# Splitting the 512-column matmuls of the weight products into two of 256 columns on the same stationary operand

## The reference

```python
def sq_relu_mlp(h, w1, w2):
    return jnp.square(jax.nn.relu(h @ w1)) @ w2

q, k, v, g, a = jnp.split(h @ w_in, split_at, axis=-1)          # first layer
z, xbc, dt = jnp.split(h @ w_in, [SSD_DI, SSD_DI + SSD_CONV_DIM], axis=-1)   # second layer
...split(h @ w_in_l, split_points, axis=-1)                     # second block, each layer
y = (jax.nn.sigmoid(g_na) * ((o_na * jax.nn.silu(z_na)) @ w_br_l[0]) + ...)
return y @ w_out_l
```

## Time and profile before

| | |
|---|---|
| runs | 2637.37, 2632.84, 2632.26 us |
| median | 2632.84 us |
| profiled execution, first to last instruction | 2625.4 us (its time with launch and end isn't listed apart) |
| TensorE matmuls | busy 2461.8 us, 94%, 13,822 instructions |
| TensorE weight loads | busy 1970.2 us, 75%, 13,822 instructions |
| VectorE, ScalarE, GpSimd | 52%, 46%, 24% |
| mean granted TensorE clock | 0.965 |
| DMA | 302.15 MB, mean 115 GB/s |

### The profile page before, as it was taken

The page is one execution under the profiler, slowest core; times in us unless marked ns, Lnnn a source line. Parts: engine busy times, 40 slices in busy tenths (PEclk is TensorE's granted clock), DMA queues, the critical chain, the costliest instruction groups (busy, mean ns, idle before and its releaser), DMA issues. The chain is left out here.

```text
span 2625.4 us, 35284 instructions
## 1 busy us (share of the span) xinstructions
PE 2461.8 (94%) x13822; PEld 1970.2 (75%) x13822; DVE 1358.5 (52%) x2133; ACT 1204.7 (46%) x2062; POOL 619.5 (24%) x376
## 2 busy tenths in 40 slices
PE   5997889999998998989999999999999999989989
PEld 3784457788888887668999767577767877768778
DVE  3206667433444767337776534552566355454675
ACT  1833334422326534445654345664357233566364
POOL 1436620000004534210001442002401115503310
PEclk8998989999999999999999999999999999999999
DMA  7235862333333433564665231222321323324335
GB/s 233 81 89 206 281 192 73 112 96 97 96 89 97 129 89 89 192 209 125 176 194 157 73 95 47 60 65 70 81 65 46 106 75 93 113 76 120 82 94 145
DMA packets 417229, 302.15 MB, mean 115 GB/s; under 512 B 10338, under 2 KB 389320, under 8 KB 417064
## 3 DMA queue, kind: packets, MB, share of 16 engines
q1 hardware_dynamic: 415952, 299.45, 38.7%
q10 hardware_dynamic: 1112, 0.44, 0.1%
HBM read 298.80 MB, written 1.05 MB: 114 GB/s over the span
## 5 line engine op out<-in xcount | busy, mean ns | idle before, releaser
L208 POOL TENSOR_TENSOR weights_lo<-wslots,weights_hi 128x1024 fp32r<-128x1024 f32 x158 | 388.2, 2466 | 857.7 <-ACT weights_hi L198 857.1
L198 ACT ACTIVATE weights_hi<-wslots 128x1024 fp32r<-128x1024 f32 x398 | 418.6, 1055 | 261.8 <-PE psum L261 215.7
L261 PE MATMUL psum<-input_hi,weights_hi 128*128 128x512 f32 (+1 forms) x1400 | 501.5, 358 | 4.4 <-PEq L855 1.8
L261 PE MATMUL psum<-input_hi,weights_lo 128*128 128x512 f32 (+1 forms) x1400 | 488.8, 349 | 0.0
L261 PE MATMUL psum<-input_lo,weights_hi 128*128 128x512 f32 (+1 forms) x1400 | 488.3, 349 | 0.0
L208 DVE TENSOR_TENSOR weights_lo<-wslots,weights_hi 128x1024 fp32r<-128x1024 f32 x240 | 296.7, 1244 | 182.4 <-ACT weights_hi L198 181.7
L261 PEld LDWEIGHTS psum<-input_hi,weights_hi 128*128 128x128 f32 x1400 | 264.7, 189 | 44.6 <-issue 7.5
L261 PEld LDWEIGHTS psum<-input_lo,weights_hi 128*128 128x128 f32 x1400 | 265.0, 189 | 38.8 <-issue 3.1
L261 PEld LDWEIGHTS psum<-input_hi,weights_lo 128*128 128x128 f32 x1400 | 264.5, 189 | 38.2
L261 PE MATMUL psum<-ffn_hidden_hi,weights_hi 128*128 128x512 f32 (+1 forms) x512 | 172.0, 336 | 0.0
L261 PE MATMUL psum<-ffn_hidden_hi,weights_lo 128*128 128x512 f32 (+1 forms) x512 | 171.7, 335 | 0.0
(11 more groups left out here) (471 smaller groups left out, 4905.2 us busy)
## 6 DMA issues: line engine op xcount, KB each, us to landing
wslots<-w_in SPq DMA_DIRECT2D x132, 512.0 KB, 4.0
wslots<-ffn_w SPq DMA_DIRECT2D x128, 512.0 KB, 4.0
wslots<-ada_w SPq DMA_DIRECT2D x96, 512.0 KB, 4.9
wslots<-ssd_w_in SPq DMA_DIRECT2D x49, 512.0 KB, 3.9
wslots<-w_ada SPq DMA_DIRECT2D x48, 512.0 KB, 4.5
wslots<-gla_w_in SPq DMA_DIRECT2D x25, 512.0 KB, 3.8
wslots<-w_br SPq DMA_DIRECT2D x24, 512.0 KB, 3.6
wslots<-ssd_w_out SPq DMA_DIRECT2D x16, 512.0 KB, 4.8
```

Of the source, the lines that this page charges most:

```text
L198: act.activation(self.part(self.whi_r, n), self.slot(n), ACT.Copy)\
L208: engine.tensor_tensor(self.part(self.wlo_r, n), self.slot(n), self.part(self.whi, n), ALU.subtract)\
L261: ins = pe.matmul(out_of(self.bank(g)), l, r, start=first and i == 0, stop=last and i == len(pairs) - 1, skip_group_check=not (first and l ...
```

## The change

In `product` and in `first_products`, a matmul whose output has 512 columns is issued as two of 256 columns: the first writes the left half of the bank's columns from the left half of the moving operand, the second the right half. Both name the same stationary operand. The start flag is on the first half of the first pair alone, the stop flag on the last half of the last pair. Matmuls of 256 columns stay as they are, and so do `part_products`, L3248, L3107 and all others.

```diff
@@ product
         if first:
             self.wait_bank(pe, g)
+        o = out_of(self.bank(g))
+        n = o.shape[-1]
+        half = n // 2 if n == 512 else n
         for i, (l, r) in enumerate(pairs):
-            ins = pe.matmul(out_of(self.bank(g)), l, r, start=first and i == 0, stop=last and i == len(pairs) - 1,
-                            skip_group_check=not (first and last))
+            for c in range(0, n, half):
+                ins = pe.matmul(o[:, c:c + half], l, r[:, c:c + half], start=first and i == 0 and c == 0,
+                                stop=last and i == len(pairs) - 1 and c + half == n, skip_group_check=True)
         if last:
             ins.then_inc(self.tick("product_done"), 1)
@@ first_products
                 xh, xl = self.input((a, e))(k)
+                half = (e - a) // 2 if e - a == 512 else e - a
                 for i, (l, r) in enumerate(((hi, xh), (hi, xl), (lo, xh))):
-                    ins = pe.matmul(self.bank(g + j)[:, a:e], l, r, start=k == 0 and i == 0, stop=k == KD - 1 and i == 2,
-                                    skip_group_check=True)
+                    for c in range(0, e - a, half):
+                        ins = pe.matmul(self.bank(g + j)[:, a + c:a + c + half], l, r[:, c:c + half],
+                                        start=k == 0 and i == 0 and c == 0,
+                                        stop=k == KD - 1 and i == 2 and a + c + half == e, skip_group_check=True)
```

## The result

| | median us (runs) | ratio to the kernel before, 95% interval |
|---|---|---|
| before, beside the changed kernel | 2633.23 (4) | |
| changed | 2652.35 (4) | 1.0078 [1.0063, 1.0093] |
| changed, measured once more | 2649.59 (6), before 2631.78 (12) | 1.0063 [1.0044, 1.0083] |

The change costs 0.6 to 0.8%, some 18 to 19 us. The forecast was 4.4 us less than before. The profiled execution has a span of 2648.7 us (its own time is 2650.5), against 2625.4.

The account below looks back on a forecast made before the run. The prediction took TensorE's matmul stream to bound the kernel. Stage terms of -1.8, +1.5 and -4.1 us summed to -4.4, taken from the 2632.8 us median to give 2628.4 us; range 2613 to 2652, likeliest case 2620 to 2638.

Parts of the forecast that it names:

- What bounds the kernel: Whole kernel: TensorE, busy 2461.8 of 2625.4 us, sets the time; changes to its matmul stream go in almost one to one.
- That the load hides behind 512 columns and is as long as 256: Split products: a full weight load takes 111 ns, hidden behind 512 columns, as long as the streaming at 256.
- The price of a pair, 230.0 ns in every stage: 4,200 split matmuls: two of 256 columns at 115.0 ns each; first layer -1.8, first feed-forward +1.5, rest -4.1 us.
- seven windows: Profile stretches of gapless 256-column matmuls before the change: three at 113.4 ns, four at 117.9, mean 115.0.
- The bounds: All 4,200 splits: -17.9 us if every pair takes 226.8 ns, +19.9 us if every pair takes 235.8.
- the slow pace throughout: Rival for all split products: every pair takes 235.8 ns, +19.9 us, 2652.7 us; chance 0.15.
- The fixed price of each extra matmul: Rival for all split products: each of 4,200 extra matmuls costs 2.6 ns, +10.9 us, 2643.7 us; chance 0.10.
- Half clock: Half-clock stretch of L280: two matmuls of 256 columns cost what one of 512 does, so no change.
- other engines: VectorE and ScalarE: weights are split well ahead and stay so at a pace that moves by 2%; zero.
- end of a product: Last pair of a product: ends after 0.395 us against 0.39, so waiting engines get it at the same time; zero.
- instruction fetch: 256-column windows already run two instructions per 113 ns without a gap for 110 us; zero.
- Lost slack at product borders: Rival at the starts of 175 tiles: each pays one more load time, +19 us less the pace's gain, 2648; chance 0.06.

## Why the prediction was wrong

**What bounds the kernel**: right. PE is at 94%, and in the first feed-forward a longer pace went into the time one to one (10.1 of 11.9 us).

**That the load hides behind 512 columns and is as long as 256**: nothing in the runs speaks against it. PEld is at 100% in the split stages, and at 128 columns and half clock the load alone holds the pace.

**The price of a pair, 230.0 ns in every stage**: this step failed. I took the mean of seven windows for all stages "because they are the same lines, operand types and slots", and held the pace to be "set anew where the stream is interrupted". All seven windows came from stages at distance 192, the one at which the fast pace is common. The first layer (792, distance 128), the first feed-forward (1,536, distance 64) and the late values by token (384, distance 64) hold 2,712 of the 4,200 splits, and neither profile of the changed kernel has it there. That one kind of stream can have two paces was right, above all at distance 192, where the same program ran the second feed-forward at 113.3 in one execution and at 117.8 in another. The sum by stage, as predicted and as the paces came out: first layer -1.8, became 792 x (237.2 - 232.3) = +3.9; first feed-forward +1.5, became +10.1; the rest -4.1. In the rest, the 384 values by token at distance 64 (235.6 a pair, against 229.2 for one before) give +2.5, and the 1,488 feature-major ones had both paces again, between 226.6 and 235.6 a pair against 233.2; over 1,859 of their 2,976 starts the mean makes 231.8 a pair in the first profile, about -2 us in all. The windows were there before the run: the 512-column rows had three levels by stage, which I averaged instead of asking what made them.

**The bounds**: the slow pace throughout, +19.9 us and 2652.7, is where the measurement lies. The first layer's 118.6 is above the slow pace of 117.9 that I had as an end, and the later stages were partly fast, so this bound met the number by luck, from a wrong description. My chance for it was 0.15.

**The fixed price of each extra matmul**: +2.6 ns by my reading, +10.9 us. Its sign was right, a fixed size was not: the same split costs +6.6 ns in one layout and +13.6 in another. The rule of the Trainium skill ("TensorE: Matmul & The Clock Gate", section "Back-to-back issue gap") has +2.5 ns for each, which makes +10.5 us; the page gives it for a matmul without its load, which the prediction doesn't say. The traces agree with neither its levels nor a fixed size.

**Half clock, other engines, end of a product, instruction fetch**: nothing in the traces speaks against the zeros. VectorE, ScalarE and GpSimd have the same busy times within 4 us.

**Lost slack at product borders**: not seen. In the first feed-forward the pace accounts for all but 1.8 us over the whole stage.

**What stays open.** The sum of the paces, 3.9 + 10.1 + 2.5 - 2, explains some 14 us of the loss. PE's busy time grew by 15.5 us in the first profile and by 20.8 in the second (the slow second feed-forward is part of that), its idle time by 7.8 and 6.8. The first 430 us grew by 8 to 10 in both profiles of the changed kernel, where the pace gives 3.9; the idle time there differs also between kernels that don't differ in that stretch (+3.9 us with the split in the first feed-forward alone, none with everything else split). Whether the split adds idle time there wasn't tried by itself. What chooses between the two paces that one layout can have is open too.

## What to carry to other kernels

When matmuls of one shape run at different paces in different stages, ask for the cause before averaging: here the distance in SBUF between the moving and the stationary operand was the main one, and moving one small tile with 64 bytes of padding took 14 us off, while the change put 18 to 19 on. A load of 128 columns of the stationary operand takes 111 ns at full clock, nearly as long as a matmul of 256 columns (113 to 120): narrower moving operands than 512 left the loads nothing to hide behind, and at 128 columns, where the clock stayed low as well, the stage took 1,330 us in place of 372. One profile shows one execution: here the pace of a stage that nobody had touched changed from one to the next.

## What the runs showed of the hardware that was not expected

- The pace of back-to-back float32r matmuls depends on the two operands' addresses: 226.5 to 234 ns at 512 columns, 113.3 to 120.1 at 256, with the distance modulo 256 bytes as the main variable: in the first feed-forward 226.7, 229, 232.4 and 233.3 at 0, 64, 128 and 192. Of it the Trainium skill ("TensorE: Matmul & The Clock Gate", section "Step-by-step: what each phase is for") says that the next tile's load doesn't take read bandwidth from the running matmul, as TensorE has two read ports. No run here measures that bandwidth. The runs show that the pace of load and matmul together depends on how the two operands' addresses lie to each other; by what mechanism, they don't show.
- One distance can hold two paces (113.3 and 117.8 at 192 and 256 columns, 229 and 233.3 at 64 and 512 columns, 118.7 and 120.0 at 128 and 256), each stable over dozens to hundreds of matmuls, and the same addresses can have one in one execution and the other in the next. What chooses between them is open.
- With 128 columns per matmul TensorE kept the lower clock, into which it had fallen at the wait before the stage, for 1,345 us on end, though PE and PEld were busy for 99% of that time (one run). With 256 or 512 columns the full clock came back at this place.
